# One layer of a hybrid decoder on one core: the start of the kernel with x loaded in column halves, scaled by quarters, and the first projection fed tile by tile

## The reference, cut to what matters

```
def rmsnorm(x, g):
    xf = x.astype(jnp.float32)
    y = xf * lax.rsqrt(jnp.mean(xf * xf, axis=-1, keepdims=True) + EPS)
    return (y * g.astype(jnp.float32)).astype(x.dtype)
...
    meta = jnp.broadcast_to(meta_tokens[None].astype(x.dtype), (b, N_META, D_MODEL))
    h = jnp.concatenate([meta, x], axis=1)
    ...
        u = rmsnorm(h, pre_mix_g[i])
        proj = u @ w_in[i]
        q, k, v, u_pool, u_conv = jnp.split(proj, splits, axis=-1)
        ... attention, pooling and convolution heads, output projection, SwiGLU FFN
```

## Time and profile before

| | us |
|---|---|
| median of 3 runs | 1129.44 |
| lowest, highest | 1127.78, 1129.67 |
| the profiled execution, device time | 1129.16 |
| its span, first to last instruction | 1127.3 |
| busy in it: PE, DVE, ACT, POOL | 1106.9, 698.1, 528.8, 21.8 |

### The profile page before, as it was taken

The page is one execution under the profiler, slowest core; times in us unless marked ns, Lnnn a source line. Parts: engine busy times, 40 slices in busy tenths (PEclk is TensorE's granted clock), DMA queues, the critical chain, the costliest instruction groups (busy, mean ns, idle before and its releaser), DMA issues.

```text
span 1127.3 us, 17681 instructions
## 1 busy us (share of the span) xinstructions
PE 1106.9 (98%) x6551; PEld 980.1 (87%) x6551; DVE 698.1 (62%) x812; ACT 528.8 (47%) x635; POOL 21.8 (2%) x39
## 2 busy tenths in 40 slices
PE   9999999999999989999999999999999999999997
PEld 8999999998888878888888888888888888888885
DVE  5599886646656766566657666666666544444444
ACT  6554444735554564444444444444444434343442
POOL 2000101101000000000000000000000000000000
PEclk9999999999999999999999999999999999999999
DMA  7655534434386266656665666566656555555553
GB/s 246 192 179 171 166 118 145 136 127 149 113 297 206 95 203 201 192 185 184 191 187 184 193 191 191 170 202 188 187 178 196 197 192 191 199 188 194 191 196 111
DMA packets 165997, 203.51 MB, mean 181 GB/s; under 512 B 6304, under 2 KB 133600, under 8 KB 165168
## 3 DMA queue, kind: packets, MB, share of 16 engines
q1 hardware_dynamic: 164800, 197.30, 55.3%
q10 hardware_dynamic: 576, 4.19, 0.9%
q0 software_dynamic: 576, 1.40, 0.4%
HBM read 200.77 MB, written 2.10 MB: 180 GB/s over the span
## 4 chain that ended last, share of the span: by engine, by line
PE 93%; DVE 3%; ACT 2%; DMA 1%; issue 1%; SPq 0%; DVEq 0%; ACTq 0%
PE ps L1063 28%; PE ps L1065 15%; PE ps L1397 7%; PE ps L1396 7%; PE ps L1395 7%; PE ps L1048 5%; PE ps L1050 5%; PE ps L1051 5%; PE ps L1303 3%; PE ps L1305 3%; PE ps L1304 3%; DVE w_lo L724 1%; DMA arena<-in_x 1%; PE ps L1161 1%; PE ps L1247 1%
## 5 line engine op out<-in xcount | busy, mean ns | idle before, releaser
L724 DVE TENSOR_TENSOR w_lo<-raw,w_hi 128x1024 fp32r<-128x1024 f32 x368 | 449.0, 1229 | 350.7 <-ACT w_hi L425 350.3
L425 ACT ACTIVATE w_hi<-raw 128x1024 fp32r<-128x1024 f32 x368 | 388.2, 1059 | 474.2 <-PE ps L1065 255.3
L1063 PE MATMUL ps<-u,w_hi 128*128 128x512 f32 x1408 | 492.8, 393 | 6.2 <-DVE w_lo L724 4.1
L1065 PE MATMUL ps<-u,w_lo 128*128 128x256 f32 x1408 | 395.5, 281 | 0.0
L1063 PEld LDWEIGHTS ps<-u,w_hi 128*128 128x128 f32 x1408 | 264.7, 188 | 66.7 <-DVE w_lo L724 4.6
L1065 PEld LDWEIGHTS ps<-u,w_lo 128*128 128x128 f32 x1408 | 266.0, 189 | 0.0
L1048 PE MATMUL ps<-u,w_hi 128*128 128x272 f32 (+1 forms) x576 | 168.3, 292 | 0.0
L1050 PE MATMUL ps<-u,w_hi 128*128 128x272 f32 (+1 forms) x576 | 165.2, 287 | 0.0
L1051 PE MATMUL ps<-u,w_lo 128*128 128x272 f32 (+1 forms) x576 | 164.9, 286 | 0.0
L1397 PE MATMUL ps<-w_hi,ffn 128*128 128x512 f32 x352 | 136.9, 389 | 0.0
L1396 PE MATMUL ps<-w_lo,ffn 128*128 128x512 f32 x352 | 136.9, 389 | 0.0
(11 more groups left out here) (174 smaller groups left out, 627.5 us busy)
## 6 DMA issues: line engine op xcount, KB each, us to landing
raw<-in_w_gate SPq DMA_DIRECT2D x88, 512.0 KB, 4.5
raw<-in_w_up SPq DMA_DIRECT2D x88, 512.0 KB, 4.4
raw<-in_w_down SPq DMA_DIRECT2D x88, 512.0 KB, 4.1
raw<-in_w_in SPq DMA_DIRECT2D x72, 512.0 KB, 3.6
raw<-in_w_out SPq DMA_DIRECT2D x32, 512.0 KB, 4.6
arena<-in_x SPq DMA_DIRECT2D x2, 1024.0 KB, 6.2
arena<-in_x ACTq DMA_DIRECT2D x2, 1024.0 KB, 9.1
out<-f_acc SPq DMA_DIRECT2D x3, 512.0 KB, 2.7
```

Source lines behind the costliest of these rows:

```text
L425: act.activation(w_hi[:, slot, :], raw[:, slot, :], ACT.Copy).then_inc(hi_done, 1)
L724: dve.tensor_tensor(w_lo[:, slot, :], raw[:, slot, :], hi_view(w_hi[:, slot, :]), ALU.subtract).then_inc(lo_done, 1)
L1063: pe.matmul(ps[:, bank + m, :].rearrange("p (a t) -> p a t", a=2), w_hi[:, slot, at], u[:, kt, :, 0:SEQ], start=first and k == 0, stop=Fal ...
L1065: mm = pe.matmul(ps[:, bank + m, 0:SEQ], w_lo[:, slot, at], u[:, kt, 0, 0:SEQ], start=False, stop=last and k == len(kts) - 1, skip_group_c ...
```

## The change

- **Loads.** Each block of x is loaded as two column halves. The load of the gain row moves from SP, behind x, to ACT's queue, as its first instruction. POOL issues its nine loads only when block 1 of x has landed.
- **Squares.** DVE sums block 0 in two halves, half of block 1 and a further quarter of it. ACT has one quarter. The parts go to `ssx`, and one TENSOR_REDUCE adds them.
- **Scaling by quarters.** Group g of four tiles needs quarter g of both blocks. ACT scales quarter 0 of block 0 first, and quarters 2 and 3 behind the last tile of groups 1 and 2; DVE does the rest.
- **First weight chunk.** ACT and DVE split chunk 0 ahead of their first tile, and chunk q ahead of group q on DVE.
- **Tile by tile.** `first_proj` does chunks 0 to 3. PE turns tiles 0 to 3, runs 10 fillers (WARM_PARTS 10, once), and then runs the six matmuls of tile kt and turns tile kt + 4, for each kt. The vector transposes come one chunk later (VEC_AT = CK = 4).

```
             for m in range(NQ):
-                sp_eng.dma_start(xr[:, m, :], x[0, m * P:(m + 1) * P, :]).then_inc(x_landed[m], 16)
-            sp_eng.dma_start(grow[0:KT, :], pre_mix_g.rearrange("a (c p) -> (a c) p", p=P)).then_inc(grow_landed, 16)
+                for cols in (slice(0, HALF), slice(HALF, D)):
+                    sp_eng.dma_start(xr[:, m, cols], x[0, m * P:(m + 1) * P, cols]).then_inc(x_landed[m], 16)
...
+            pool.wait_ge(x_landed[1], 32)
             at = 0
             for v in (mix_out_g, pre_ffn_g, pool_scale, b_dw, conv_ln_g, conv_ln_b):
...
+            def scaled(m, n):
+                cols = slice(n * QUART, (n + 1) * QUART)
+                act.activation(xs[:, m, cols], xr[:, m, cols], ACT.Copy, scale=r0[:, m:m + 1]).then_inc(xs_act, 1)
+
             act.wait_ge(r0_done, 2)
-            act.activation(xs[:, 1, 0:D // 2], xr[:, 1, 0:D // 2], ACT.Copy, scale=r0[:, 1:2]).then_inc(xs_act, 1)
+            scaled(0, 0)
             act.wait_ge(grow_turned, 1)
             act.copy(vec[:, 0:KT], ps[:, 0, 0:KT]).then_inc(grow_done, 1)
+            split(0)
             act.wait_ge(grow_done, 1)
             for kt in range(KT):
                 act.wait_ge(u_made, kt + 1)
                 act.activation(u[:, kt, 0, :], ps[:, 4 + kt % 4, 0:TOK], ACT.Copy,
                                scale=vec[:, V_PRE + kt:V_PRE + kt + 1]).then_inc(u_hi, 1)
-                if kt % CK == CK - 1:
-                    split(kt // CK)
+                if kt == CK - 1:
+                    split(1)
+                elif kt % CK == CK - 1 and kt < KT - 1:
+                    scaled(0, kt // CK + 1)
+                    split(kt // CK + 1)
...
+            part_squares(0, slice(0, HALF), 0, 32)
+            part_squares(0, slice(HALF, D), 1, 32)
+            part_squares(1, slice(0, HALF), 0, 32)
+            part_squares(1, slice(HALF, 3 * QUART), 1, 32)
...
+            def turn_rows(kt):
+
+                if kt % CK == 0:
+                    pe.wait_ge(xs_dve, (1, 3, 4, 5)[kt // CK])
+                    pe.wait_ge(xs_act, (2, 2, 3, 4)[kt // CK])
+                if kt >= 4:
+                    pe.wait_ge(u_lo, kt - 3)
...
+            def first_proj(outs):
+
+                for kt in range(KT):
+                    q, k = kt // CK, kt % CK
+                    if k == 0:
+                        pe.wait_ge(lo_done, q + 1)
+                    pe.wait_ge(u_lo, kt + 1)
...
+                    if k == CK - 1:
+                        mm.then_inc(chunks_used, 1)
+                    if kt + CK < KT:
+                        turn_rows(kt + CK)
```

More of the change, by code:

```diff
@@ L728, in split, with part_squares, scaled @@
                 split_lo(q, q % WSLOTS)
[L731 to L737, removed]
-            dve.wait_ge(ss_act, 2)
-            dve.tensor_tensor(ss0[:, 1:2], ss0[:, 1:2], sst[:, 0:1], ALU.add).then_inc(ss_dve, 1)
+            def part_squares(m, cols, n, landed):
+                dve.wait_ge(x_landed[m], landed)
+                dve.scalar_tensor_tensor(xs[:, m, cols], xr[:, m, cols], 1.0, xr[:, m, cols], ALU.mult, ALU.mult,
+                                         accum_out=ssx[:, m, n:n + 1]).then_inc(ss_dve, 1)
+            part_squares(0, slice(0, HALF), 0, 32)
+            part_squares(0, slice(HALF, D), 1, 32)
+            part_squares(1, slice(0, HALF), 0, 32)
+            part_squares(1, slice(HALF, 3 * QUART), 1, 32)
+            dve.wait_ge(ss_dve, 4)
+            dve.wait_ge(ss_act, 2)
+            dve.wait_ge(const_step, 7)
+            dve.tensor_reduce(ss0[:, 0:2], ssx, AX.X, ALU.add).then_inc(ss_dve, 1)
+            def scaled(m, n):
+                cols = slice(n * QUART, (n + 1) * QUART)
+                dve.tensor_scalar(xs[:, m, cols], xr[:, m, cols], r0[:, m:m + 1], None, ALU.mult).then_inc(xs_dve, 1)
             dve.wait_ge(r0_done, 2)
-            for m, n in ((0, 0), (0, 1), (1, 1)):
-                half = slice(n * D // 2, (n + 1) * D // 2)
-                dve.tensor_scalar(xs[:, m, half], xr[:, m, half], r0[:, m:m + 1], None, ALU.mult).then_inc(xs_dve, 1)
+            scaled(1, 0)
+            scaled(0, 1)
+            scaled(1, 1)
             for kt in range(KT):
+                if kt % CK == 0:
+                    split(kt // CK)
+                if kt in (CK, 2 * CK):
+                    scaled(1, kt // CK + 1)
                 dve.wait_ge(u_hi, kt + 1)
@@ L1097, in _ @@
             keep_warm(WARM_ROWS)
[L1099 to L1113, removed]
+            def turn_rows(kt):
+                if kt % CK == 0:
+                    pe.wait_ge(xs_dve, (1, 3, 4, 5)[kt // CK])
+                    pe.wait_ge(xs_act, (2, 2, 3, 4)[kt // CK])
+                if kt >= 4:
+                    pe.wait_ge(u_lo, kt - 3)
+                b, cols = 4 + kt % 4, slice(kt * P, (kt + 1) * P)
+                pe.transpose(ps[:, b, 0:META], xsm[0:META, cols], ident[0:META, 0:META])
+                pe.transpose(ps[:, b, META:META + P], xs[:, 0, cols], ident)
+                pe.transpose(ps[:, b, META + P:TOK], xs[:, 1, cols], ident).then_inc(u_made, 1)
+            for kt in range(CK):
+                turn_rows(kt)
             keep_warm(WARM_PARTS)
             def early_work(q):
[L1117 to L1120, removed]
                 if q == VEC_AT:
@@ L1126, in early_work @@
                                  ident[0:TAPS * CT, 0:TAPS * CT]).then_inc(vec_turned, 1)
+            def first_proj(outs):
[4 more added lines that the diff above has]
+                    pe.wait_ge(u_lo, kt + 1)
+                    x_hi, x_lo = normed(kt)
+                    for m in range(2):
+                        at = slice(k * BLK + m * P, k * BLK + (m + 1) * P)
+                        pe.matmul(outs[m], w_hi[:, q, at], x_hi, start=kt == 0, stop=False, skip_group_check=True)
+                        pe.matmul(outs[m], w_hi[:, q, at], x_lo, start=False, stop=False, skip_group_check=True)
+                        mm = pe.matmul(outs[m], w_lo[:, q, at], x_hi, start=False, stop=kt == KT - 1,
+                                       skip_group_check=True)
+                    if k == CK - 1:
+                        mm.then_inc(chunks_used, 1)
+                    if kt + CK < KT:
+                        turn_rows(kt + CK)
             def proj(q0, outs, one_bank=False, lo=0):
@@ L1137, in _ @@
                     pe.wait_ge(a_kept, i)
-                proj(i * 2 * CK + Q_CONV, wide(0))
+                    proj(i * 2 * CK + Q_CONV, wide(0))
+                else:
+                    first_proj(wide(0))
                 if i:
```

20 lines of the change are left out of this document (11 added, 9 removed).

## The result

The changed kernel took 1134.88 us, median of five runs (1133.14 to 1135.6), beside 1129.51 for the kernel before (five runs, 1127.78 to 1130.83) run beside it: a ratio of 1.0045 (95% interval 1.0033 to 1.0057), slower by 5.4 us. The prediction said 1131.2 with a range of 1129.0 to 1133.2, so the sign was among its cases but the size lies outside. The profiled execution of after is the quickest of its five, 1133.14 with a span of 1131.3, against 1129.16 and 1127.3 before: 4.0 us of span have to be found.

The account below looks back on a forecast made before the run. PE was taken to bound the kernel, busy without a wait from 12.42 us to the end of chunk 3. +0.66 - 0.51 + 0.45 + 1.24 = +1.84 on 1129.16 gave 1131.0; forecast 1131.2, own range 1130.4 to 1132.0, with rivals 1129.0 to 1133.2.

Parts of the forecast that it names:

- the sign: Whole kernel's time: slower than 1131.7 us chance 0.36, faster than 1127.2 chance 0.05, within chance 0.59.
- What bounds the kernel: PE, start to end of chunk 3: busy without a wait from 12.42 us, so its delay there moves the whole kernel.
- The arrival of x: Loads at the start: x complete at 9.07 us as before, change zero, with 0.3 to either side.
- The squares: DVE's sums of squares at the start: half of block 1 plus a further quarter, +0.66 us.
- the scaling: ACT ahead of PE's first tile: a quarter to scale instead of a half, 1.16 becomes about 0.65, -0.51 us.
- The first tile at 12.57: PE's first turned tile: 12.42 + 0.66 - 0.51 = 12.57 us.
- The fillers: PE behind tiles 0 to 3: one piece of 10 instead of two of 4, 2.23 against 1.78 us, +0.45.
- Two waits: PE at tiles 8 and 12, for ACT's scaling of quarters 2 and 3: 0.62 us each, +1.24 for both.
- The joints: PE's changes between matmuls and transposes, 3 pairs becoming 12: taken as 0, upper end 1.7 us.
- the rival with 1.7: PE, chunks 0 to 3: twelve met waits between matmuls and transposes each cost up to 0.14 us, 1132.9; chance 0.07.
- The clock rival: PE around its first transposes: no plain matmul until 14.7 us, clock falls, 1.7 us lost, 1132.9; chance 0.14.
- The fall at 400 us fails to come: PE behind its 3.5 us wait near 400 us: clock stays up, 1.7 us saved, 1129.5; chance 0.17.

Follow-up runs that it names:

- the last version: Changed kernel with x loaded whole, quarters 2 and 3 scaled one group earlier, block 1's squares by halves, 5 fillers: 1128.38 us, ratio 0.9990; again 1128.27, 0.9991.
- the second profile: Changed kernel, unaltered, run and profiled once more: median 1133.80 us, ratio 1.0040 against the kernel before.

## Why the prediction was wrong, step by step

**What bounds the kernel: right.** PE without a hole from the first tile to chunk 3, so only the first tile's time, the fillers and new waits count; the differences up to chunk 4 make up the span's whole difference.

**The arrival of x: the step that failed.** "I take zero for the arrival of x, with 0.3 to either side." It was +0.9 in the profile of after, +0.55 in the second, and up to +1.7 in other kernels with halves. The step priced the neighbours of x's loads, POOL's packets, rightly at nothing, but it did not price the loads themselves, although they were what the diff changed. The trace of before had no halves to read a price from, and the right answer to that was a wider bound upward. At SP's pitch of 0.47 between issues two more loads put the last issue 0.94 later; that was in reach from the queue's own timeline and would have set such a bound. That it is the size that came in this profile is in part luck, since other kernels with the same last issue lost 0.55 to 1.7. The sentence on the Trainium skill's "DMA: Bandwidth & Descriptors", section "Measured (HBM→SBUF, 128 partitions, SWDGE, issued from GpSimd)", spoke in the right direction: from 3 to 8 us whole blocks moved at 386 GB/s, halves at 338. Its 341 GB/s for 1 MB is not the same case, and that the numbers agree is chance.

**The squares, +0.66, and the scaling, -0.51: right**, measured +0.60 and -0.43. The quarter on ACT takes 0.73, more than the 512-column rows that stood as its neighbours.

**The first tile at 12.57:** 13.49, wrong by x alone.

**The fillers, +0.45: right as work**, 2.23 us wherever the clock was up (five profiles), and more than was needed: five were enough in the last version, with no wait behind them.

**Two waits, +1.24: right in place, number and cause, mis-sized by 0.28.** They were 0.48 each. ACT is free 0.38 after it begins a single tile (24.64 to 25.02); the step took 0.49, from four tiles in a row, and that is 0.11 of the 0.14 by which each wait came out shorter.

**The joints, 0: right**, 0.1 in all; the rival with 1.7 is out.

**The clock rival, chance 0.14: it came**, in the profiled execution, for 1.6 us (1.7 was its price). What decided it was not as it said. Transposes do hold the clock up; what let it fall was PE standing 1.88 us, and that gap was long only because x was late. The prediction had treated this rival as independent of x, and had an idle time of 1.4 in mind (11.2 to 12.57); the nearest that was seen, 1.19, did not lower the clock. The failed step and the rival were one event: x late by 0.9 costs 0.9, and with some chance 1.6 more. That is also why the range was too narrow: no case in it had both. By itself neither would have left it.

**The fall at 400 us fails to come, chance 0.17:** it was absent in one profile of the last version and there in the next, and before's own times leave a gap of 1.2 us behind the quickest, so it is not the change that decides it. Its price of 1.7 was a little high, since PE was still waiting for a part of the low stretch: from the end of the wait to the end of the span before took 726.6, and the two kernels that kept the clock 725.2, so 1.4.

The sum redone with measured terms, for an execution with the fall: 0.90 + 0.60 - 0.43 + 0.27 + 1.76 + 0.96 + 0.1 = 4.16, beside 4.18 read. Without it, with the first tile of the second profile, 0.73 + 0.45 + 0.96 + 0.1 = 2.24, beside 37.44 - 35.19 = 2.25. The profiled execution of after, 1133.14 us, lies just inside the range; it is the median, 1134.88, that does not. The differences of the medians, 5.4 and 4.4 us, are 1.2 and 0.2 above the first of the two sums. The profiled executions are among the quicker ones of ten (1131.6 to 1135.6), x in halves came as late as 10.8 in other kernels, and the fall at 400 us cost 1.4 to 3.0 where it came, so a later x or a longer fall in the typical execution would explain the rest; no profile of such an execution exists, and this part is argued. What is shown is that it goes away with the two repairs: with x whole and the quarters scaled earlier the median is 1129.74, 0.3 from before's.

## What to carry to other kernels

A gain in when an engine's input is ready is worth nothing if that engine has other work to do until then; ask first where its holes are. Cutting a load into pieces so that work can start on the first has a price on the last: here two more loads delayed the complete pair of blocks by 0.55 to 1.7 us, and nothing used the early piece. When two risks hang on the same cause (late data, a gap, a lower clock), add them in one case instead of giving each its own.

## What the runs showed of the hardware

- The way a block is cut into loads goes with its rate. From 3 to 8 us, with the engines 90% busy or more, blocks of 128 rows x 8 KB moved at 380 to 397 GB/s (six profiles), the same in column halves at 289 to 347 (six), in column quarters at 285 and in 64-row halves at 236 (one each). In a shorter stretch the ranges touch: from 4.5 to 6 us it was 388 to 426 whole and 284 to 396 in halves.
- Twelve fp32 transposes in a gap kept the granted clock at 1.00 as well as sixteen more plain matmuls did; standing 1.88 to 2.08 us was followed by a clock of 0.50 for some 3.4 us, standing 1.19 was not.
- Behind one and the same 3.45 us wait at 400 us the clock stayed up in two of fourteen profiles; in ten its fall cost 1.4 to 1.7 us, and in two 2.75 and 3.0. One profile shows one of these cases.
- The first 52 fillers at the very start took 7.62 to 9.00 us in different executions, so that in one of them PE reached the first tile later than x did.
